# Gate columns in pairs with seven block products for eight, block stores on two queues, a convolution in two parts

## The reference, cut to what matters

```python
h = rms_norm(x, norm_pre)
(aq, ak, av, az, dq, dk, dv, db, da, dz, gate_att, gate_dn) = split_cols(h @ w_in)
y_att = (o_att * silu(az)) @ w_br_att
qkv = silu(short_conv(concat(dq, dk, dv), conv_w))     # five taps along the tokens
o_dn = rms_norm(delta(q, k, v, g, beta, forwards) + delta(..., backwards))
y_dn = (o_dn * silu(dz)) @ w_br_dn
mix = (sigmoid(gate_att) * y_att + sigmoid(gate_dn) * y_dn) @ w_out
```

## Time and profile before

| what | value |
|---|---|
| three timed runs | 3263.31, 3266.35, 3268.90 us |
| profiled execution, its own time | 3268.52 us |
| its span, first to last instruction | 3266.7 us |
| TensorE matmuls busy | 3016.7 us (92%) |
| TensorE weight loads busy | 2466.8 us (76%) |
| VectorE busy | 2044.6 us (63%) |
| ScalarE busy | 1408.0 us (43%) |
| GpSimd busy | 1175.9 us (36%) |
| mean granted TensorE clock | 0.971 of 2.4 GHz |
| matmuls of the two branch stages (L2779) | 1745.8 to 2010 us and 2805.7 to 3066.5 us of the span |

### The profile page before, as it was taken

One profiled execution on the slowest core, in us unless ns is written; L12 is line 12 of the kernel. 1 busy time (PEld: TensorE's weight loads), 2 busy tenths in 40 slices (PEclk: granted clock), 3 DMA queues, 4 the chain that ended last, 5 costly groups with the idle time before them and its releaser, 6 DMA issues. The chain is left out here.

```text
span 3266.7 us, 43916 instructions
## 1 busy us (share of the span) xinstructions
PE 3016.7 (92%) x16017; PEld 2466.8 (76%) x16017; DVE 2044.6 (63%) x3738; ACT 1408.0 (43%) x2790; POOL 1175.9 (36%) x1306
## 2 busy tenths in 40 slices
PE   7999989989999899798999999997989888999998
PEld 5678867756887667587887887787877788788787
DVE  6889976576998756676773004677857788301244
ACT  3356557224664661335663211455434553321232
POOL 5226532232363223522004242235443445524331
PEclk8999999989999999899999999999999999999999
DMA  8422333541233245410002124124241232412342
GB/s 294 136 55 84 116 107 103 166 162 51 69 97 108 93 137 168 133 52 1 1 6 90 51 62 144 29 53 99 71 123 39 65 94 76 163 47 102 116 155 71
DMA packets 229609, 309.41 MB, mean 95 GB/s; under 512 B 41199, under 2 KB 142447, under 8 KB 227217
## 3 DMA queue, kind: packets, MB, share of 16 engines
q1 hardware_dynamic: 217874, 285.62, 28.7%
q10 hardware_dynamic: 11520, 20.98, 1.8%
HBM read 244.01 MB, written 62.52 MB: 94 GB/s over the span
## 5 line engine op out<-in xcount | busy, mean ns | idle before, releaser
L1027 PE MATMUL psum<-qs,hT 128*128 128x512 f32 x1248 | 284.5, 389 | 1.4 <-POOL qs L1112 1.4
L1027 PEld LDWEIGHTS psum<-qs,hT 128*128 128x128 f32 x1248 | 233.8, 188 | 51.8 <-POOL qs L1112 3.5
L2779 PE MATMUL psum<-bhsn,bringn 128*128 128x512 f32 x1056 | 241.1, 390 | 2.4 <-DVE bhsn L2861 1.5
L2779 PE MATMUL psum<-bhsa,bringa 128*128 128x512 f32 x1056 | 240.1, 389 | 2.9 <-POOL bringa L2840 2.9
L2779 PEld LDWEIGHTS psum<-bhsn,bringn 128*128 128x128 f32 x1056 | 197.9, 188 | 45.2 <-DVE bmixn L2901 2.2
L2779 PEld LDWEIGHTS psum<-bhsa,bringa 128*128 128x128 f32 x1056 | 198.1, 188 | 44.4 <-issue 3.3
L3158 PE MATMUL psum<-hTs,cws 128*128 128x512 f32 x960 | 230.2, 396 | 0.0
L3158 PEld LDWEIGHTS psum<-hTs,cws 128*128 128x128 f32 x960 | 179.3, 190 | 36.3
L1192 DVE TENSOR_SCALAR_CACHE_REDUCE junk<-score,cand 128x384 uint8<-128x384 f32 x248 | 186.8, 810 | 2.2
L1907 PE MATMUL psum<-w_out,oys 128*128 128x512 f32 x768 | 181.1, 398 | 6.9 <-POOL oys L1974 4.7
L1907 PEld LDWEIGHTS psum<-w_out,oys 128*128 128x128 f32 x768 | 147.1, 192 | 41.1 <-POOL oys L1974 5.9
(11 more groups left out here) (564 smaller groups left out, 7134.0 us busy)
## 6 DMA issues: line engine op xcount, KB each, us to landing
stg<-in_w_in SPq DMA_DIRECT2D x88, 256.0 KB, 2.7
score<-in_w_ada SPq DMA_DIRECT2D x32, 512.0 KB, 4.3
pj<-ptmp ACTq DMA_DIRECT2D x64, 256.0 KB, 2.1
dlb<-blocks SPq DMA_DIRECT2D x32, 512.0 KB
dlb<-in_w_in SPq DMA_DIRECT2D x20, 512.0 KB, 3.9
wa<-in_w_ada SPq DMA_DIRECT2D x8, 1024.0 KB, 12.7
ostg<-in_w_out SPq DMA_DIRECT2D x16, 512.0 KB, 6.0
x<-ozb SPq DMA_DIRECT2D x16, 512.0 KB, 3.0
```

Of the source, the lines that this page charges most:

```text
L1027: mm = pe.matmul(bank(m), lhs, rhs, start=(first and x == 0), stop=(last and x == 2))
L2779: mm = pe.matmul(ps[:, m, :], w[:, a, fs], h, start=(j == 0 and x == 0), stop=(j == KC - 1 and x == 2))
```

## The change

**Branch stages.** The two gate passes (2 x 192 matmuls) are replaced by four pairs of 128-column groups. In a pair, the product of a weight matrix cut in 2 x 2 blocks (halves of the 1024 rows by two column groups of 128) with `h` cut in 2 x 2 blocks (halves of its rows by halves of the tokens) is done with seven block products for eight (the Winograd form). A block product is four row chunks by three matmuls, 12 matmuls into one bank. Sums of the `h` blocks (`T13`, `T4`, and one in place of the late half of `hs` for chunks 0 to 3) are made once by VectorE (`make_t`), with high parts by ScalarE (`t_hi`). Sums of the weight blocks are made for each pair by VectorE (`weight_sums`, `last_weight_sum`). After the products VectorE adds the partial results (`after_second`, `after_third`, `after_last`), ScalarE keeps two of them and takes the sigmoids (`keep`, `activate`). Since the `h` sums take the memory of `bmix`, the gates are stored to a DRAM tensor `gated` tile by tile and come back with one load of 4 MB after the last product. The row chunks of `h` are loaded nine more times each stage (chunk 0, then all eight for the sums) through four buffers for two; there are two `btmp` buffers for three.

**Delta stages.** For step 0, three of the eight stores of `dnlx` stay on SyncE's queue and five are issued by ScalarE, in column 9 of the convolution before its second half is emptied; the load of direction 0's blocks waits only for the second-last column's weights. The last convolution's three first taps stay at the end of round -1, and the two last taps go behind `attend(2, 0)` of round 0. `decay(3, 0)` moves behind `merge_last(0, 1)`.

The diff, cut to its core:

```diff
@@ stage_branch
+    HK, PROD, PAIRS = KC // 2, 7, 4
+    RING, STAGING, LEAD, TMP, U, HST = 4, 3, 2, 2, 8, 4
+    F_A11, F_S2, F_S1, F_A12, F_S3, F_S4, F_A22 = range(PROD)
@@ sync
+            for n, i in ((KC + 1, 0), (KC + 3, 1), (KC + 4, 2), (KC + 5, 3)):
+                for v in range(KC + 2 if i == 1 else n, n + 1):
+                    load_silu(v)
+                if i == 2:
+                    load_pair(0)
+                for kc in (i, i + HK):
+                    load_chunk(chunk(kc, True))
+            for n in range(KC + 6, PAIR0):
+                load_silu(n)
+            load_pair(1)
+            load_pair(2)
+            store_gates(0)
+            load_pair(3)
+            store_gates(1)
+            for n in range(BR0, ITEMS):
...
+                load_slice(n, wbr[:, kc, (c - 2) * HALF:(c - 1) * HALF])
+                if n == BR0 + STAGING - 1:
+                    store_gates(PAIRS - 2)
+                if n == BR0 + STAGING + 1:
+                    store_gates(PAIRS - 1)
+                    sp.wait_ge(s_prod, PROD * PAIRS)
+                    for q in range(2):
+                        sp.wait_ge(s_gst[q], 128)
+                    sp.dma_start(mixT[:, :, :], t["gated"]).then_inc(s_gl, 16)
@@ tensor
+            def product(n):
+                j, p = pair_of(n)
...
+                for kc in range(HK):
+                    for i, (a, b) in enumerate(((0, 0), (0, 1), (1, 0))):
+                        mm = pe.matmul(ps[:, bank, :], ring[:, n % RING, a, kc * P:(kc + 1) * P], moving(p, b, kc),
...
+                mm.then_inc(s_prod, 1)
@@ scalar
+            def after(n):
+                j, p = pair_of(n)
+                if p in (F_A11, F_S1):
+                    keep(j, p)
+                if p == F_S3:
+                    activate(j, 0)
+                    activate(j, 1)
+                if p == F_S4:
+                    activate(j, 2)
+                if p == F_A22:
+                    activate(j, 3)
+            for n in range(DONE, ITEMS):
+                hi(n)
+                if KC + RING <= n < PAIR0:
+                    t_hi(n - KC - RING)
+                if n in (KC - 1 + LEAD, PAIR0 - 1 + LEAD):
+                    for m in range(U):
+                        silu(U * (n // KC - 1) + m)
+                if PAIR0 <= n - LEAD < BR0:
+                    after(n - LEAD)
@@ vector
+            for j in range(PAIRS):
+                after_second(j)
+                last_weight_sum(j)
+                if j == PAIRS - 1:
...
+                    for kc in range(HK):
+                        y_hi(kc)
+                after_third(j)
+                if j + 1 < PAIRS:
+                    weight_sums(j + 1)
+                after_last(j)
+            for kc in range(HK, KC):
+                y_hi(kc)
@@ stage_conv, sync
-                store_blocks(sp, t, sc, st, 1, sc.NLx)
-                if st == 0:
-                    sp.wait_ge(s_wlo, C - BASE)
-                    for r in range(2):
-                        load_blocks(sp, t, sc, 0, r, sc.Lb)
+                if st:
+                    store_blocks(sp, t, sc, st, 1, sc.NLx)
+                    continue
+                store_blocks(sp, t, sc, 0, 1, sc.NLx, BY_SP)
+                sp.wait_ge(s_wlo, C - BASE - 1)
+                load_blocks(sp, t, sc, 0, 0, sc.Lb)
+                sp.wait_ge(s_wlo, C - BASE)
+                load_blocks(sp, t, sc, 0, 1, sc.Lb)
@@ stage_conv, scalar
+                    if half and c == 9:
+                        act.wait_ge(sc.s_NLx, 1)
+                        store_blocks(act, t, sc, 0, 1, sc.NLx, BY_ACT)
@@ stage_delta, scalar, round 0
                     last.silu(last.column)
-                    decay(3, 0)
                     keep_x(0, 0, 1)
...
                     merge_last(0, 1)
+                    decay(3, 0)
                     decay(3, 1)
@@ stage_delta, vector
-                    last.convolve(last.column)
+                    last.begin_convolve(last.column)
                     continue
...
                     attend(2, 0)
+                    last.end_convolve(last.column)
                     decayed(2, 1)
```

More of the change, by code:

```diff
@@ L2658, in stage_branch @@
     tag = "n" if mix_in is not None else "a"
[L2659 to L2663, removed]
+    HK, PROD, PAIRS = KC // 2, 7, 4
+    RING, STAGING, LEAD, TMP, U, HST = 4, 3, 2, 2, 8, 4
+    PAIR0, BR0 = 2 * KC, 2 * KC + PROD * PAIRS
+    ITEMS = BR0 + 2 * KC
+    DONE = 1
     LOADED = 2 if mix_in is not None else DONE
     mix_last = k.mix_last[0 if mix_in is None else 1]
+    F_A11, F_S2, F_S1, F_A12, F_S3, F_S4, F_A22 = range(PROD)
@@ L2669, in stage_branch @@
         ring = k.sb(ctx, f"bring{tag}", [P, RING, 2, HALF], F32R)
[L2670 to L2676, removed]
+        raw = [k.sb(ctx, f"braw{i}{tag}", [P, 2, HK, 2, P]) for i in range(2)]
@@ L2710, in _, with load_slice, load_chunk @@
             wbr = w_branch[0].rearrange("(k p) n -> p k n", p=P)
[L2711 to L2714, removed]
+            def load_slice(n, src):
+                q = staged.index(n)
+                sp.dma_start(stage_slot(n), src).then_inc(s_w[q % STAGING], 16)
+            def load_chunk(i):
+                if i >= HST:
+                    past, again = chunks[i - HST]
+                    if again:
+                        sp.wait_ge(s_T, past % HK + 1)
+                    elif past:
+                        sp.wait_ge(s_hlo, past + 1 - DONE)
+                    else:
+                        sp.wait_ge(s_h0, 1)
+                sp.dma_start(hst[i % HST][:, :], t["hTd"][:, chunks[i][0], :]).then_inc(s_h[i % HST], 16)
@@ L2723, in _ @@
[L2723 to L2728, removed]
-                        sp.dma_start(yT[:, f, :], y_in[:, f, :]).then_inc(s_y[f // 4], 16)
@@ new lines, in _ @@
+            for n in range(LOADED, KC):
+                if y_in is not None and n == HG:
+                    sp.wait_ge(k.od_last[0], 32)
+                    sp.wait_ge(k.od_last[1], 32)
+                load_chunk(chunk(n, False))
+                load_silu(n)
+                if y_in is not None and n >= HG:
+                    for f in range(2 * (n - HG), 2 * (n - HG) + 2):
+                        sp.dma_start(yT[:, f, :], y_in[:, f, :]).then_inc(s_y[f // 4], 16)
+            load_chunk(chunk(0, False))
@@ L2784, in _ @@
                     mm.then_inc(s_used, 1)
+            for n in range(ITEMS):
+                if PAIR0 <= n < BR0:
+                    product(n)
+                else:
+                    piece(n)
         @block.scalar
         def _(act):
[L2788 to L2802 removed]
@@ L2851, in _, with h_hi @@
         def _(dve):
-            for kc in range(DONE, KC):
-                raw = chunk_in(dve, kc)
-                if first and kc == first.w_chunk:
+            link = chainer(dve, s_ch)
+            def h_hi(kc):
+                if kc < LOADED:
+                    dve.wait_ge(k.next_h1, 16)
+                    src = first.h1_in
+                else:
+                    src = wait_chunk(dve, kc)
+                if kc == first.w_chunk:
                     dve.wait_ge(s_used, 1)
```

417 lines of the change are left out of this document (311 added, 106 removed).

## The result

The changed kernel takes 3249.02 us (median of 4 runs, 3245.57 to 3253.54) against 3265.35 us before (4 runs): a ratio of 0.995, 95% interval 0.9938 to 0.9963, or -16.3 us. Five more runs of it later gave 0.9935 (0.9921 to 0.9949), -19.0 us. The forecast was 3241.0 (-25.4) with a range of 3232 to 3255: the time lies inside the range and is 8 us longer than forecast.

What follows compares the result with a forecast made beforehand. TensorE was taken to bound the gate passes and VectorE the delta stages. Gates -18.4 us (-21.8 + 2.4 + 1.0) and delta stages -7.0 make -25.4, from the median 3266.35 to 3241 us; range 3232 to 3255.

Steps and rivals of the forecast that it cites:

- Part 1, removed matmuls: Gate passes of both branch stages: 48 matmuls fewer at 0.2266 us each, 10.9 us a stage, 21.8 for both.
- The chain: Gate products: sums through VectorE, ScalarE and GpSimd nearly keep up with TensorE; 0.3 us lost a pair, 1.2 a stage.
- Rival 1: Gate products: ScalarE, GpSimd and VectorE do not keep up, each of eight pairs loses 2 us: 3254.5 us, chance 0.14.
- Part 1, late loads: Delta branch: the attention result's load issued about 8 us later; first slice and multiplications late, 1.0 us lost, bounds 0 and 4.
- Rival 4: Branch stages: the 4 MB gates load is slow and the sixth slice 26 us late in each: 3293 us, chance 0.05.
- Part 2, block stores: Start of each scan: shared stores and earlier loads gain 2.4 to 3.1 us (heads 0 to 3) and 1.4 (4 to 7).
- cap 3.1: Heads 0 to 3: block-load gain limited to 3.1 us because column 10's convolution must await its copied input; heads 4 to 7, 1.5.
- Part 2, the last convolution: Round 0: splitting it brings the turn of step 1 earlier by 0.9 to 1.7 us, heads 4 to 7 1.5 to 2.3.
- turned at E+16.2: Round 0: turn of step 1 comes 16.2 us after convolution end E, B+26.5 to 27.3, B being the last convolution's begin.
- then as before from the turned tile: Round 0, after silu at E+1.1: the stretch to `merge_last`'s end takes 7.0 us, as in the earlier trace.
- Rival 3: Scans: VectorE and not the mask sets the turn of step 1, 5 us more gained: 3236 us, chance 0.07.
- rival 2: Delta stages: the scans give back what their starts gain, leaving -18.4 us: 3248 us, chance 0.14.

Runs made afterwards that it cites:

- gated_halves: The changed kernel with the 4 MB load of the gates in two halves, the second in the last branch pass: 3237.75 us, 0.9925 of the kernel before.
- conv_only: The kernel before with only the last convolution in two parts and `decay(3, 0)` behind `merge_last`: 3261.35 us, ratio 0.9997.
- conv_whole: The changed kernel with the last convolution back in one piece and `decay(3, 0)` in its old place: 3238.47 us, 0.9929 of the kernel before.
- solve_late: The changed kernel with the first two solve columns of step 1 moved behind the two `merge32`: 3242.09 us, 0.9941 of the kernel before.
- scans_only: The kernel before with only the edits of the delta stages, its branch stages kept: 3255.68 us, ratio 0.9988.
- after: The changed kernel, whole, in its first measurement against the kernel before: 3249.02 us, ratio 0.995.
- after_again: The changed kernel itself, unchanged, run again beside the kernel before: 3242.35 us, ratio 0.9935.
- widen_first: The changed kernel with GpSimd's widening of step 1 ahead of the two masks of step 3 in round 0: 3243.28 us, 0.9942 of the kernel before.
- before: The kernel without the change, the base of all ratios: 3265.35 us beside the changed kernel; 3260.6, 3262.9 and 3261.4 in the three later groups.
- stores_only: The kernel before with only the block stores of step 0 shared and each load waiting for its own last weights: 3254.14 us, ratio 0.9978.
- gates_only: The kernel before with only the new branch stages, its delta stages kept: 3248.27 us, ratio 0.9964.

## Why the prediction came out as it did

**Part 1, removed matmuls: right.** 10.9 us a stage were forecast, by 48 matmuls fewer at 0.2266 us each. The gate parts last 77.2 and 77.6 us for the forecast 76.1. **The chain: right size, other shape.** 1.2 a stage were forecast as 0.3 in each pair. Measured: one stall of 0.75 and 0.70 at the first sum, and 0.3 and 0.8 more in slightly longer products (T4's matmuls in the delta branch 396 ns for 389). Rival 1 is out. The prediction put the rule of the Trainium skill ("SBUF — State Buffer", "SBUF: two separate sides") at 11 us less, one whole low part lost in each of eight pairs (8 x 1.3 is 10.4). That didn't come: TensorE's stalls in this part are 1.5 us in both stages together. The rule itself isn't refuted by it. Four of GpSimd's 27 low parts of weights in each gate part took 1.8 us for 1.29, and in the delta branch one of VectorE's sums 1.80 for 0.95: meetings were few, and TensorE stalled at none but the first sum.

**Part 1, late loads: mechanism right, term mis-sized.** "the first slice of the last pass comes some 0.4 us late and the multiplications some 0.6: 1.0 us". The load of the result was 8.6 us later (29.5 us into the first branch pass for 21.0), 8 were forecast. The slice came 0.82 late and the multiplications' stalls grew from 0.73 to 2.65: 2.7 in all for the 1.0. gated_halves takes 4.9 of the 8.6 us away and the stage falls by 2.5. The delta branch stage brought 6.5 us, 8.7 were forecast, the attention branch stage 10.0 at full clock, 9.7 forecast. Rival 4 is out: the two loads of the gates landed 12.1 and 12.4 us after their issue, and the slice behind the second was there 13 us after it.

**Part 2, block stores: under-estimated.** Forecast 2.4 to 3.1 and 1.4, measured 3.3 in each scan. The step that failed is "cap 3.1", and the cap of 1.5 for heads 4 to 7: the copies of the earlier trace rows that I read as the input of column 10 are the first half of column 11. In the kernel before column 10's two halves are copied 21.9 and 19.1 us before the turn of step 0 (heads 4 to 7: 20.3 and 17.5), and its convolution begins 9.7 before it in every trace, behind the solve. No copy capped the gain. Why the landing moved by 3.3 and not by the 2.4 and 1.4 of the last weights was not followed.

**Part 2, the last convolution: wrong.** Forecast 0.9 to 1.7 and 1.5 to 2.3; conv_only and conv_whole measured no gain. Of the chain "turned at E+16.2" three links held: convolved at B+10.1 (10.3 to 11.1 forecast), from `merge_last` to the last exp 5.1 us (5.1), from there to the turn 2.6 (3.0). The link that failed is the 7.0 us "then as before from the turned tile": from silu's end at E+1.1, which the turn of the last column now follows at once, to the end of `merge_last` it took 9.2 to 10.3, not 7.0. I carried over a length from another order of the queues. Now two solve columns stand on VectorE behind `decayed` and `attend` and fall together with GpSimd's `scale_rows`, short operations of 0.27 us become 1.0 to 1.3, and the merges that ScalarE and TensorE wait for stand behind them. With these columns out of the way (solve_late) the link is 8.5 and 7.1 us: all of the excess in heads 4 to 7, about half of it in heads 0 to 3, where the rest is not explained. Rival 3, VectorE setting the turn, is out by 5.5 us; what rival 2 had in mind, scans that give their starts back, is true of the convolution alone.

**The sum.** Part 2 came out at 4.9 us (scans_only) for the 7.0 taken. That it came so near is luck: the stores brought some 2.3 more than the 4.2 in it, the convolution about 3 less, and the two errors cancel in part. By stages of these traces: 9.4 (attention branch, mean of ten traces against four) + 6.5 (delta branch) + 6.5 (stores) + 0 = 22 us. The medians say 16.3 and 19.0. The 3 to 6 us between are open. Stages in which nothing was changed differ by as much from run to run; in the projections ahead of heads 0 to 3 the profiled execution of after lost some 5 us against after_again, of which a granted clock of 0.77 for 0.89 in 15 us explains at most 1.8:

```profile
2084.20:2099.20 15.00, 11.46 (x50) 0.77 0.13 37
```

## What to carry to other kernels

Follow a moved operation through its queue neighbours: here a turn that waited for a mask waited in truth for an exp, for a copy, and for four short operations in front of a transpose. What one engine gains at a hand-over is worth only as much as the slowest of the queues behind it; widen_first lost most of its 4.4 us a scan to two loads behind two others on SyncE, and putting them first kept all of it. Check by its count which unit a row belongs to before it becomes a bound of a sum.

## What the runs showed of the hardware

Short VectorE operations with two SBUF inputs (128x120, 0.27 us alone) take 1.0 to 1.3 us while GpSimd runs its 128x512 ones of 1.27, and each of the three ends 0.12 to 0.14 us behind one of GpSimd's. That is about one whole GpSimd operation each, which in this stretch is what the Trainium skill says ("SBUF — State Buffer", "SBUF: two separate sides"). In solve_late they come after GpSimd's last one (it ended at 2197.75) and take 0.28.

TensorE's granted clock at the start of the attention branch stage was 1.00 in before, stores_only and after_again, and 0.50 to 0.69 over the first 4 us in gates_only, conv_only, after and scans_only; that alone moves the stage by 1.2 to 3 us. In before and in gates_only TensorE had done the same work just ahead of it (busy 2.95 us of one stretch of 4, 3.05 and 3.19 of the next, then idle for some 2).
